# A hybrid HGRN2 and gMLP block on 8 cores: gates taken a turn ahead, attention steps a group later, sums on GpSimd

## The chip, the cores and the metric

One Trainium2 chip, all 8 cores, one launch. Each core computes half a sequence (1024 of 2048 positions) of one of 4 batch rows. The time is the device time of the slowest core in microseconds.

## What is computed

```python
h = rmsnorm(x, norm_mix)
q, f_pre, inp, g, u, v, gate_a, gate_b = split(h @ w_in)      # 4 x 1024, 2 x 1024, 2 x 2048 columns
f = lb + (1 - lb) * sigmoid(f_pre)                            # HGRN2: 8 heads of 128, state 128 x 128
o = hgrn2_scan(silu(q), 1 - f, inp, log(f))                   # S_t = diag(f_t) S_{t-1} + k_t v_t^T, o_t = S_t^T q_t
y_a = (rmsnorm(o) * silu(g)) @ w_a_out
y_b = (gelu(u) * gmlp_spatial(layernorm(gelu(v)))) @ w_b_out  # W_s mixes 128 positions, 8 heads
x = x + (sigmoid(gate_a) * y_a + sigmoid(gate_b) * y_b) @ w_o
x = x + relu(rmsnorm(x) @ w_ff1) ** 2 @ w_ff2                 # 2048 -> 8192 -> 2048
x = x + sigmoid(rmsnorm(x) @ w_ple_gate) * (p @ w_ple_proj)
return rmsnorm(x)
```

A core with the second half of a sequence also needs the state at its start. It gets it from the first half's x (`xpT`, zeros on the other cores), whose forget gates and values it computes too.

## The kernel before

The program is written out by hand, engine by engine, with one semaphore per engine: `X.after(event)` is a wait until that event of engine X, and each engine carries out its own list strictly in order. Activations lie transposed, 16 chunks of 128 features by 1024 positions; a half `hf` is 512 positions. A matrix product is cut into groups of 16 matmuls (one per chunk `c`) that fill one of 8 PSUM banks of 128x512. Weights are stored as float32 and arrive as bfloat16 through GpSimd's DMA queue (`load`, L1135) in four slots of 4096 columns; a slot's next load waits until TensorE (PE) has used it (`frees`). The loads of x go through SyncE's queue.

The stages, in order:

- **Start.** x comes in 9 pieces (L1188). For each chunk VectorE (DVE) makes the bfloat16 product with the gain (`raw`, L852), ScalarE (ACT) squares each half into `SQ[hf]` (L626, one buffer per half), and DVE adds the square to `ACC` (`accumulate`, L843). PE runs the first 8 `u` groups chunk by chunk (L353) as x arrives, then the other 8 group by group; after the first of these come the two matmuls that sum the squares over partitions (`total("x", 4)`, L341). `rstd` (L635, L638) turns this into the norm factor. Then DVE writes the normalised x (`normalise`, L861, 32 pieces) and after every second piece scales one `u` group (`u_scale`, L871), in the order of `UG`, that is groups 0 to 7 first; ACT takes the gelu (L650). The `u` groups of n = 6, 7 reuse banks of n = 4, 5.
- **V.** 8 value groups `V(1, i)` and 8 `V(0, i)` from the normalised x (L409). During `V(1, i)` the first half's x lands, piece by piece after the normalised pieces 2i+1 of half 1, and is squared and summed as before. Then `total("xp")`, and `V(2, i)`.
- **Heads.** `mixer_order` writes a list that all engines walk through. Step X has 8 groups k (two each of fp, f, q, g for head X). Between them stand the small steps of the heads a = X-2 and b = X-1. At k = 4: `on` (sum of squares of the head's output, PE L491, in banks 4 and 5), `decay` (4 exponentials on ACT, 3 products on DVE), `onorm` (ln, exp, products; L719 to L723 on ACT), `logf` (2 logarithms, 2 scans of 2.3 us, L964 and L969). Then the transposes `tk`, `tkp` (L442), the masked products `attn` (masks on DVE, L992 and L994), `kv` (a chain of 7 small DVE products and 8 small GpSimd products, L1007 and L1157). The small steps take turns between banks 4 and 5, and each waits until the engine that reads the step two before it has freed the bank (`take`). In the list of ACT a step's copy stands where the step stands.
- **v groups.** Steps X = 8 and 9 have no head groups; their 16 places hold the v groups (i, a) of the gMLP, with `vn` (layer norm on DVE with a short hop to GpSimd: L1018, L1020, L1162, L1164, L1022) once both halves a of a position block i are there, `bt` (bias terms, PE L496, DVE L1033), and `sp` (spatial products, PE L380; DVE L917 and L923). Behind them follow `gate(0, 0, 0)`, `gate(0, 0, 1)`, 4 spatial steps of the second half, `gate(0, 1, 0)`, 4 more, `gate(0, 1, 1)`. The first of these spatial steps waits for `vn` of i = 7.
- **Merge, w_o, the MLP** (L442 to L572): not touched.
- **Last stage.** 32 turns t (half by half): PE does the 16 matmuls of `pg` (L597) and 2 of `pp`; DVE scales the gate (L1111), ACT takes the sigmoid (L814), DVE multiplies (L1114) and adds (L1117), ACT squares (L626), DVE sums (L843). DVE waits for the sigmoid in each turn. `finish` (L1098) scales the output, half 0 beside the turns of half 1, half 1 at the end, and SyncE stores it (L1203).

## Time and profile before

| | us |
|---|---|
| runs: median (lowest to highest) | 2046.86 (2044.54 to 2274.42), 3 runs |
| the profiled execution, its own time | 2047.13 |
| its span on the slowest core (5) | 2045.8 |
| spans of the 8 cores | 2033.6 to 2045.8 |
| busy in it: PE, DVE, ACT, GpSimd | 1947.7, 688.8, 573.1, 111.6 |

The span is the time from the first to the last instruction of a core; outside it lie 1.3 us of the execution's own time. The granted clock is the share of TensorE's full speed (2.4 GHz) that the chip allowed; 0.5 is its lower level (1.2 GHz). In the windows, a stretch whose PE is busy for less than its length has waits of PE in it.

### The profile page before, as it was taken

Reading aid. Unit: us, or ns where it says so; the run is one execution under the profiler, and the core shown is the slowest. Engines: PE = TensorE matmul, PEld = TensorE weight load, DVE = VectorE, ACT = ScalarE, POOL = GpSimd, SP = SyncE. Lnnn points to the kernel's source line nnn. Section 1 sums busy time; section 2 is a strip of 40 time slices with the busy share of each in tenths; the row PEclk is TensorE's granted clock in tenths of the full one; section 3 lists DMA queues with packets and bytes.
Section 4 is the critical chain, followed back from the end, with each engine's and each line's share of the span. In section 5 each row is a group of like instructions: output and inputs, shape, how many; then the busy total and the mean of one; then the engine's idle time right before and its main releaser. Section 6 shows DMA issues by size and latency. Waiting matters only on the chain.

```text
span 2045.8 us, 25263 instructions; the slowest of 8 cores (2033.6 to 2045.8 us)
## 1 busy us (share of the span) xinstructions
PE 1947.7 (95%) x9300; PEld 891.6 (44%) x9300; DVE 688.8 (34%) x1042; ACT 573.1 (28%) x886; POOL 111.6 (5%) x235
## 2 busy tenths in 40 slices
PE   5799989998899999999999999999999999999993
PEld 2344444444444444444444444444444444444441
DVE  4760455246531222223312122121222112233667
ACT  3453465445211111123432003300231013333332
POOL 1000001011100000000000000000000000000000
PEclk9899999999899999999999999999999999999997
DMA  9851314142374434354434434434443444563304
GB/s 223 180 126 31 62 32 73 27 83 52 52 177 102 91 64 85 70 124 83 73 72 83 79 68 81 83 68 77 83 74 71 82 81 76 101 124 67 58 21 144
DMA packets 33127, 174.04 MB, mean 85 GB/s; under 512 B 3056, under 2 KB 3184, under 8 KB 18032
## 3 DMA queue, kind: packets, MB, share of 16 engines
q0 software_dynamic: 21872, 138.16, 37.3%
q1 hardware_dynamic: 11136, 34.26, 5.2%
q8 instruction: 78, 1.28, 0.3%
q14 instruction: 41, 0.34, 0.1%
HBM read 302.17 MB, written 8.39 MB: 152 GB/s over the span
## 4 chain that ended last, share of the span: by engine, by line
PE 87%; DVE 4%; DMA 3%; ACT 3%; issue 2%; SPq 0%; DVEq 0%; ACTq 0%; POOL 0%; POOLq 0%
PE ps L572 49%; PE ps L333 27%; PE ps L409 5%; DMA RX<-xT 2%; PE ps L597 2%; PE ps L432 2%; DMA RW<-wb 1%; DVE RX L1098 1%; DVE RP L1114 1%; ACT RP L814 1%; DVE RC L843 1%; DVE RH L861 1%; DVE RP L1111 0%; PE ps L442 0%; ACT L708 0%
## 5 line engine op out<-in xcount | busy, mean ns | idle before, releaser
L572 PE MATMUL ps<-RH,RW 128*128 128x512 bf16 x2048 | 442.8, 379 | 0.0
L333 PE MATMUL ps<-RH,RW 128*128 128x512 bf16 x1792 | 409.9, 383 | 5.7 <-DMA RW<-wb 5.7
L572 PE MATMUL ps<-RP,RW 128*128 128x512 bf16 x1536 | 332.0, 379 | 0.0
L572 PEld LDWEIGHTS ps<-RH,RW 128*128 128x128 bf16 x2048 | 200.4, 98 | 241.6
L333 PEld LDWEIGHTS ps<-RH,RW 128*128 128x128 bf16 x1792 | 175.4, 99 | 213.5 <-issue 14.1
L1071 DVE TENSOR_TENSOR RX<-RX,ps 128x512 f32<-128x512 f32 x160 | 110.1, 688 | 406.5 <-PE ps L572 406.5
L572 PEld LDWEIGHTS ps<-RP,RW 128*128 128x128 bf16 x1536 | 150.3, 98 | 181.2
L572 PE MATMUL ps<-RQ,RW 128*128 128x512 bf16 x1024 | 221.3, 379 | 0.0
L800 ACT ACTIVATE ps<-ps 128x512 f32<-128x512 f32 x128 | 74.5, 582 | 502.8 <-PE ps L572 502.8
L1089 DVE TENSOR_TENSOR ps<-ps,RC 128x512 f32<-128x512 f32 x128 | 89.6, 700 | 353.2 <-ACT ps L800 353.2
L626 ACT ACTIVATE RC<-RX 128x512 bf16<-128x512 f32 (+1 forms) x160 | 99.3, 629 | 259.4 <-DVE RC L843 226.4
L1135 POOL DMA_DIRECT2D RW<-wb x136 | 73.3, 540 | 1698.5 <-PE ps L572 924.5
L572 PEld LDWEIGHTS ps<-RQ,RW 128*128 128x128 bf16 x1024 | 100.2, 98 | 120.8
L333 PE MATMUL ps<-RQ,RW 128*128 128x512 bf16 x512 | 120.5, 379 | 0.0
L774 ACT ACTIVATE RX<-ps 128x512 f32<-128x512 f32 x64 | 38.2, 597 | 290.2 <-PE ps L333 290.2
L843 DVE TENSOR_TENSOR RC<-RC 128x512 f32<-128x512 f32 x150 | 100.1, 685 | 6.2 <-ACT RC L626 6.2
L333 PE MATMUL ps<-RP,RW 128*128 128x512 bf16 x384 | 87.8, 386 | 13.0 <-ACT RQ L650 11.5
L333 PEld LDWEIGHTS ps<-RQ,RW 128*128 128x128 bf16 x512 | 50.1, 98 | 60.4
L1051 DVE TENSOR_TENSOR RX<-RX,ps 128x512 f32<-128x512 f32 x32 | 22.0, 688 | 136.5 <-PE ps L333 136.1
L333 PEld LDWEIGHTS ps<-RP,RW 128*128 128x128 bf16 x384 | 37.4, 99 | 57.5 <-issue 16.7
L432 PE MATMUL ps<-RW,RH 128*128 128x512 bf16 x256 | 59.5, 387 | 1.3 <-DMA RW<-wb 1.3
L1048 DVE TENSOR_TENSOR RX<-RX,ps 128x512 f32<-128x512 f32 x32 | 22.0, 688 | 110.5 <-PE ps L333 110.5
(135 smaller groups left out, 1301.0 us busy)
## 6 DMA issues: line engine op xcount, KB each, us to landing
RW<-wb POOLq DMA_DIRECT2D x112, 1024.0 KB, 8.0
RW<-wb POOLq DMA_DIRECT2D x24, 512.0 KB, 10.1
RX<-xT SPq DMA_DIRECT2D x8, 1024.0 KB, 33.2
RX<-xpT SPq DMA_DIRECT2D x8, 1024.0 KB, 13.1
outT<-RX SPq DMA_DIRECT2D x16, 512.0 KB, 4.0
RX<-xT SPq DMA_DIRECT2D x2, 2048.0 KB, 18.4
RX<-xT SPq DMA_DIRECT2D x2, 1536.0 KB, 39.4
RP<-wb POOLq DMA_DIRECT2D x3, 1024.0 KB, 13.5
```

What stands on the lines that cost most here:

```text
L333: ins = e.matmul(out, w3[:, c, cs], src[:, c, ts], start=c == 0, stop=c == kc - 1)
L409: ins = e.matmul(PS[bank][:, :], src[:, c, i * 128:(i + 1) * 128], wide[c // 8][:, c % 8, :], start=c == 0, stop=c == 15)
L432: ins = e.matmul(PS[bank][:, :], HT[:, c, i * 128:(i + 1) * 128], wide[c // 8][:, c % 8, :], start=c == 0, stop=c == 15)
L572: ins = e.matmul(PS[b + hf][:, :], w3[:, c, (n % 2) * 128:(n % 2 + 1) * 128], src[:, c, half(hf)], start=c == 0, stop=c == 15)
L597: ins = e.matmul(PS[b][:, :], w3[:, c, (n % 2) * 128:(n % 2 + 1) * 128], HT[:, c, half(hf)], start=c == 0, stop=c == 15)
L626: e.activation(out=SQ[hf] if n else ACC[:, half(hf)], in_=XT[:, n, half(hf)], func=AF.Square, scale=D ** -0.5).then_inc(*ACT.on("sq", tag, ...
L774: e.activation(out=TMPA[2 * g + k], in_=PS[b0 + 2 * k][:, :], func=AF.Sigmoid).then_inc(*ACT.on("sg" + name, n, hf))
L800: e.activation(out=pb, in_=pb, func=AF.Relu).then_inc(*ACT.on("relu", q, n, hf))
L843: e.tensor_tensor(out=SQ[hf] if n == 15 else acc, in0=acc, in1=SQ[hf], op=ALU.add).then_inc(*DVE.on("acc", tag, n, hf))
L1071: e.tensor_tensor(out=XT[:, n, half(hf)], in0=XT[:, n, half(hf)], in1=PS[b_of(n) + hf][:, :], op=ALU.add).then_inc(*DVE.on("xadd", tag, n, ...
L1089: e.tensor_tensor(out=pb, in0=pb, in1=RSTD[:, half(hf)], op=ALU.mult).then_inc(*DVE.on("hr", q, n, hf))
L1135: e.dma_start(out=c3(WS[j % NSLOT][:, 0:n], 2048), in_=c3(wb_d[blk][:, 0:n], 2048)).then_inc(*WL[j % NSLOT].on("w", j))
```

## The change

- **Last stage:** the gate's scaling and its sigmoid are issued one turn ahead, on DVE and on ACT. Three `finish` that stood behind the turns go into turns 28 to 31, the sum of half 0 is totalled a turn later, and ACT calls a logarithm before its last wait.
- **Start:** the first two weight blocks are cut by rows (1024 rows by 512 columns), so that they are loaded in 4 transfers instead of 8. The sums of half 1 of x run on GpSimd. Blocks 2 and 3 are issued after GpSimd's tenth sum instead of upon x's chunks 10 and 11, block 2 in two halves. `total("x")` stands before the second 8 `u` groups and waits for GpSimd. The `u` groups are scaled in a new order (`U_TURN`: the first is group (4, 0)), one after each of the first 16 normalised pieces.
- **V:** the first half's x is squared beside `V(0, i)` instead of `V(1, i)`, and its total stands after `V(2, 0)`.
- **Heads:** `tk`, `tkp`, `spre` stand one group later, `attn(b, 0)` directly behind `tkp`; `kv`, `intra` and `inter` go in pairs; at k = 4 the order is `ek` (the first exponential), `oln` (the logarithms of `onorm`), the rest of `decay`, the rest of `onorm`, `logf`.
- **v groups:** the values go four by four (i = 0 to 3 with a = 0, then a = 1, then i = 4 to 7), with four buffers instead of two; `bt` stands at places 6 and 7 instead of 2 and 3, and `sp` at 9, 10 and 12 to 15.

```diff
@@ weight_blocks, mixer_order @@
-    for j in range(4):
+    for k in range(2):
+        blks.append(("w_in", k * 1024, 1024, [(4096, 512)]))
+    for j in range(2, 4):
         blks.append(("w_in", 0, D, [(4096 + j * 256, 256)]))
...
-    values = [(0, 0), (1, 0), (0, 1), (1, 1)] + [(i, a) for i in range(2, 8) for a in range(2)]
+    values = [(i + j, a) for i in (0, 4) for a in range(2) for j in range(4)]
...
-                out += [[("attn", a, 1), ("kv", a, 0)], [("kv", a, 1), ("intra", a, 0)], [("intra", a, 1), ("inter", a, 0)],
-                        [("inter", a, 1), ("sqo", a)], [("on", a)], [], [], []][k]
+                out += [[("spre", a), ("attn", a, 1)], [("kv", a, 0), ("kv", a, 1)], [("intra", a, 0), ("intra", a, 1)],
+                        [("inter", a, 0), ("inter", a, 1), ("sqo", a)], [("on", a)], [], [], []][k]
             if k == 4:
+                if 0 <= b < NH:
+                    out.append(("ek", b))
+                if 0 <= a < NH:
+                    out.append(("oln", a))
...
-                out += [[], [], [], [], [], [("tk", b)], [("tkp", b)], [("spre", b), ("attn", b, 0)]][k]
+                out += [[], [], [], [], [], [], [("tk", b)], [("tkp", b), ("attn", b, 0)]][k]
...
-                if g in (2, 3):
-                    out.append(("bt", g - 2))
-                if g >= 9:
-                    out += [("sp", g - 9, 0)] + [("sp", 7, 0)] * (g == 15)
+                if g in (6, 7):
+                    out.append(("bt", g - 6))
+                out += [("sp", h, 0) for h in {9: (0,), 10: (1,), 12: (2,), 13: (3, 4), 14: (5, 6), 15: (7,)}.get(g, ())]
@@ emit @@
-    BT = rxf(2048)
+    BT = rxf(6144)
-    GVT = [RP[:, 4096 + i * 2048:4096 + (i + 1) * 2048].bitcast(F32) for i in range(2)]
+    GVT = [RP[:, 4096 + i * 2048:4096 + (i + 1) * 2048].bitcast(F32) for i in range(2)] + [rxf(5120), rxf(2048)]
+    U_TURN = [g for pair in zip(UG[8:], UG[4:8] + UG[:4]) for g in pair]
@@ pe_program @@
-                e.wait_ge(*DVE.after("acc", tag, 15, hf))
+                e.wait_ge(*(POOL if tag == "x" and hf else DVE).after("acc", tag, 15, hf))
...
             for n, hf in UG[:8]:
-                w3 = c3(slot("u", n // 2), 256)
-                ins = e.matmul(PS[BANK["u", n, hf]][:, :], w3[:, c, (n % 2) * 128:(n % 2 + 1) * 128], RPv[:, c, half(hf)],
+                ins = e.matmul(PS[BANK["u", n, hf]][:, :], w3[:, c % 8, n * 128:(n + 1) * 128], RPv[:, c, half(hf)],
...
+        total("x", 0)
+        for n, hf in UG[8:]:
...
+                if (n, hf) == (4, 0) and c % 8 == 0:
+                    e.wait_ge(*U2L[c // 8].after("w"))
...
-            if k == 0:
-                total("x", 4)
...
-                if grp == 2 and i == 0:
+                if grp == 2 and i == 1:
                     total("xp", 6)
...
-                if (n, hf) == (1, 1):
+                if (n, hf) == (2, 1):
                     total("pg", 6, (0,))
@@ act_program @@
+        for n, hf in UG[:4]:
+            raw_u(n, hf)
+        rstd("x", 0, RSTDH)
+        for n, hf in UG[4:8]:
+            raw_u(n, hf)
+        for n, hf in U_TURN:
...
-                if grp == 1:
+                if grp == 0:
                     e.wait_ge(*XPL[i].after("x"))
...
+            elif kind == "ek":
...
                 e.activation(out=EK, in_=BBM, func=AF.Exp, scale=-1.0).then_inc(*ACT.on("ek", h))
+            elif kind == "decay":
...
+            elif kind == "oln":
...
-                if i >= 2:
-                    e.wait_ge(*DVE.after("vn", i - 2))
+                if i >= 4:
+                    e.wait_ge(*DVE.after("vn", i - 4))
+                elif (i, a) == (2, 0):
+                    e.wait_ge(*DVE.after("khtp", 6))
...
+        def sigmoid(t):
+            e.wait_ge(*DVE.after("gt1", t % 16, t // 16))
+            e.activation(out=GT[t % 2], in_=GT[t % 2], func=AF.Sigmoid).then_inc(*ACT.on("gts", t % 16, t // 16))
+
+        sigmoid(0)
...
+                if t < 31:
+                    sigmoid(t + 1)
                 e.wait_ge(*DVE.after("xadd", "pg", n, hf))
                 square("pg", n, hf)
...
+        e.activation(out=MISC[:, 3:4], in_=EPSC, func=AF.Ln).then_inc(*ACT.on("ln_table"))
         rstd("pg", 6, RSTDH, ("gt1", 15), (1,))
@@ dve_program @@
-            for hf in range(2):
-                if c >= 2:
-                    accumulate("x", c - 1, hf)
-        for hf in range(2):
-            accumulate("x", 15, hf)
+            if c >= 2:
+                accumulate("x", c - 1, 0)
+        accumulate("x", 15, 0)
...
-                if c % 2:
-                    u_scale(*todo.pop(0))
+                if hf == 0:
+                    u_scale(*U_TURN[c])
...
-                if c:
-                    accumulate("xp", c, hf)
+                if c >= 3:
+                    accumulate("xp", c - 2, hf)
+        for c in (14, 15):
+            for hf in range(2):
+                accumulate("xp", c, hf)
...
+        def gate(t):
+            n, hf = t % 16, t // 16
+            gt = GT[t % 2]
+            e.wait_ge(*PE.after("pg", n, hf))
+            if t >= 2:
+                e.wait_ge(*DVE.after("xadd", "pg", (t - 2) % 16, (t - 2) // 16))
+            e.tensor_tensor(out=gt, in0=PS[((16 * 9 + t) % 3) * 2][:, :], in1=RSTD[:, half(hf)], op=ALU.mult).then_inc(
+                *DVE.on("gt1", n, hf))
...
+        gate(0)
+        for t in range(32):
...
+            if t < 31:
+                gate(t + 1)
+            e.wait_ge(*ACT.after("gts", n, hf))
+            e.wait_ge(*PE.after("pp", n, hf))
...
+            if t >= 20:
+                finish(t - 20, 0)
+            if t >= 28:
+                finish(t - 16, 0)
+        accumulate("pg", 15, 1)
         for c in range(16):
             finish(c, 1)
@@ pool_program, sp_program @@
+        def accumulate_x(n):
+
+            e.wait_ge(*ACT.after("sq", "x", n, 1))
+            if n >= 2:
+                e.wait_ge(*POOL.after("acc", "x", n - 1, 1))
+            e.tensor_tensor(out=SQ[1] if n == 15 else ACC[:, 512:1024], in0=ACC[:, 512:1024], in1=SQ[1], op=ALU.add).then_inc(
+                *POOL.on("acc", "x", n, 1))
...
-            for j in range(2):
-                e.dma_start(out=WS[j][:, cols], in_=wb_d[j][:, cols]).then_inc(*UL[j][p].on("w"))
-        e.wait_ge(*XL[piece_of(11)].after("x"))
-        for j in range(2, 8):
+            cols = slice((p % 2) * 2048, (p % 2 + 1) * 2048)
+            e.dma_start(out=WS[p // 2][:, cols], in_=wb_d[p // 2][:, cols]).then_inc(*UL[p].on("w"))
+        for n in range(1, 11):
+            accumulate_x(n)
+        for p in range(2):
+            cols = slice(p * 2048, (p + 1) * 2048)
+            e.dma_start(out=WS[2][:, cols], in_=wb_d[2][:, cols]).then_inc(*U2L[p].on("w"))
+        load(3)
+        for n in range(11, 16):
+            accumulate_x(n)
+        for j in range(4, 8):
             load(j)
...
-        e.wait_ge(*DVE.after("khtp", 6))
+        e.wait_ge(*DVE.after("kt", 7))
         e.dma_start(out=BT, in_=bass.AP(bsp_d.tensor, 0, [[0, 128], [1, 1024]])).then_inc(*BSPL.on("bsp"))
```

## Rows read from the trace of the kernel before

**Rows 1.** The profile's page: busy time, share of the span and instructions of each engine
```profile
PE 1947.7 (95%) x9300; PEld 891.6 (44%) x9300; DVE 688.8 (34%) x1042; ACT 573.1 (28%) x886; POOL 111.6 (5%) x235
```
**Rows 2.** Windows: stretch, length, then busy time of each engine, clock, DMA
```profile
54.50:101.80 47.30, 34.24 (x147) 14.69 (x148) 34.78 (x54) 20.45 (x33) 1.59 (x3) 0.86 0.83 180
...
516.00:572.00 56.00, 46.62 (x272) 23.11 (x269) 33.32 (x57) 14.29 (x21) 8.66 (x21) 0.91 0.33 57
...
2013.00:2045.80 32.80, 0.80 (x2) 0.10 (x1) 22.84 (x35) 6.38 (x9) 0.00 (x0) 0.58 0.54 192
```
**Rows 3.** Waits of PE, whole span: us in total, times, longest
```profile
PE ps L442 <- ACT RC L719: 13.2, 5, 2.9
PE ps L333 <- ACT RQ L650: 11.5, 1, 11.5
...
PE ps L333 <- DMA RW<-wb: 5.7, 1, 5.7
```
**Rows 4.** Timeline of the start: start, us, engine, line [idle before <- releaser]
```profile
41.22 0.75 DVE L852 TENSOR_SCALAR RP<-RX,RC 128x1024 bf16<-128x1024 f32 x1 [2.30 <-DMA RX<-xT]
...
44.22 1.07 POOL L1135 DMA_DIRECT2D RW<-wb  x2 [38.26 <-DMA RX<-xT]
...
57.00 1.23 ACT L626 ACTIVATE RC<-RX 128x512 bf16<-128x512 f32 x2 [0.63 <-DVE RC L843]
...
59.84 3.61 PE L333 MATMUL ps<-RP,RW 128*128 128x512 bf16 x16 [1.50 <-ACT RQ L646]
```
**Rows 5.** Timeline, normalised pieces and the wait in the u groups
```profile
67.45 1.42 DVE L861 SCALAR_TENSOR_TENSOR RH<-RX,RC 128x512 bf16<-128x512 f32 x2 [8.35 <-ACT RC L638]
...
85.72 6.58 PE L333 MATMUL ps<-RP,RW 128*128 128x512 bf16 x20 [11.48 <-ACT RQ L650]
```
**Rows 6.** GpSimd's own operations by source line: ns min/median/max
```profile
L1157 POOL TENSOR_SCALAR RX<-RX x64: 371/372/380, 245.9 to 524.5; 128x128 bf16<-128x128 f32 x64
...
L1162 POOL TENSOR_TENSOR RC<-RC x8: 184/189/192, 495.3 to 555.7; 128x1 f32<-128x1 f32 x8
```
**Rows 7.** Timeline of a head step, from its group k = 4
```profile
259.96 0.59 PE L491 MATMUL ps<-RC 128*128 128x512 bf16 x2
...
260.83 1.28 ACT L708 ACT_TABLE_LOAD   x1
...
266.87 0.55 PE L442 MATMUL ps<-RC,RX 128*128 128x128 bf16 x7 [2.87 <-ACT RC L719]
...
267.26 5.30 PE L333 MATMUL ps<-RH,RW 128*128 128x512 bf16 x16
...
271.73 0.91 ACT L747 ACTIVATE RX<-ps 128x896 bf16<-128x896 bf16 x1
```
**Rows 8.** Timeline of the v groups: the on step, a vn on DVE, the last gate
```profile
498.39 0.61 PE L491 MATMUL ps<-RC 128*128 128x512 bf16 x2 [2.17 <-DVE RX L1033]
...
505.65 1.28 DVE L1018 BATCH_NORM_STATS2 RC<-RP 128x6 f32<-128x512 f32 x2
...
508.37 0.81 DVE L1022 TENSOR_SCALAR RP<-RP,RC 128x1024 bf16<-128x1024 f32 x1 [1.13 <-POOL RC L1164]
...
571.76 3.40 PE L333 MATMUL ps<-RH,RW 128*128 128x512 bf16 x15
```
**Rows 9.** Timeline of the last turns and the end
```profile
2012.65 0.68 DVE L1111 TENSOR_TENSOR RP<-ps,RC 128x512 f32<-128x512 f32 x1
...
2014.23 0.69 DVE L1114 TENSOR_TENSOR RP<-RP,ps 128x512 f32<-128x512 f32 x1 [0.90 <-ACT RP L814]
...
2016.96 0.68 DVE L1111 TENSOR_TENSOR RP<-ps,RC 128x512 f32<-128x512 f32 x1
...
2025.90 0.69 DVE L843 TENSOR_TENSOR RC<-RC 128x512 bf16<-128x512 f32 x1 [0.23 <-ACT RC L626]
...
2030.55 10.69 DVE L1098 SCALAR_TENSOR_TENSOR RX<-RX,RC 128x512 f32<-128x512 f32 x16 [1.97 <-ACT RC L638]
```

76 lines of the change are left out of this document (32 added, 44 removed).

## The prediction

> **What bounds the kernel now.** The page first: PE is busy for 1947.7 of 2045.8 us [rows 1], so about 98 us can be had at most, and the matmuls themselves are untouched. Then the windows, to see where PE waits: 13.1 us of 47.3 between 54.5 and 101.8, 9.4 between 516 and 572, and 32.0 behind the last turn [rows 2]. The waits of PE give the causes: a bank that a gelu has not freed (11.5), the attention transposes that wait for the logarithms of `onorm` (5 times, 13.2 in all), one late weight block (5.7) [rows 3]; the timeline adds 2.17 for `bt` ahead of `on` at X = 8 [rows 8]. Half as dear again is the clock: after a wait of 2.87 us a group took 5.30 instead of 3.61 [rows 7], after the one of 11.48 us 20 matmuls took 6.58 [rows 5] where 16 take 3.61 and 15 take 3.40 [rows 4, 8], which makes 0.215 a matmul and 3.45 from one group's start to the next; that wait cost 6.58 - 20 x 0.215 = 2.3 us more. All sums below are made on the profiled execution (2047.1, 1.3 of it outside the span), which lies 0.3 above the median of the runs.
>
> **Last stage.** A turn takes DVE 2016.96 - 2012.65 = 4.31 us; in it the second product starts 1.58 us after the first because the sigmoid lies between [rows 9]. PE needs 18 matmuls, 3.88, so DVE falls behind through half 1. With the sigmoid a turn ahead the product follows after about 0.64 (two instructions of 512 columns that wait for nothing take 1.28, [rows 8]) and the turn takes 4.31 - 1.58 + 0.64 = 3.37: DVE keeps up, and turns 28 to 31, which take a `finish` (0.67, 16 in 10.69) more, are 0.15 over PE, 0.4 us in all. PE's last gate ends at about 2012.6, as DVE had been waiting for no one. From there stand before the last sum: scaling 0.64, product 0.86, add 0.64, sum 0.64, two `finish` 1.34, then product 0.86, add 0.64, sum 0.64, two `finish` 1.34, together 7.6, so it starts at 2020.2 + 0.4 instead of 2025.90 [rows 9]. The early logarithm takes a table load of 1.28 [rows 7] off what follows. The 16 `finish` and the last store stay. **Gain 6.6**; the ends are 0 (the new order makes the product of turn t wait for the matmuls of t + 1, and ACT could trail) and 8.
>
> **Start.** The wait of 11.48 [rows 5] goes: group (4, 0) is now scaled first, straight after the first normalised piece, and its bank is asked for only 4 groups (13.8 us) after the total, while the path from total to normalise takes about 4 and scaling and gelu with table 0.7 + 1.3 + 0.6 more. DVE has the same 48 instructions, in another order; V's first group needs the 16th piece 31 us after the total, and DVE, which now waits for PE's u groups in between, has it at 30. So nothing is late there. The wait and its slow clock are worth 11.5 + 2.3 = 13.8.
>
> New is GpSimd's chain. ACT may not square the next chunk's half 1 before GpSimd has added the last one (one buffer). A square takes 0.6 (two in 1.23, [rows 4]). GpSimd's addition of two 512 inputs is not in the trace. Its own operations take 189 ns for one element and 372 for 128 [rows 6], so one input of 512 would take 0.93, two read in turn 1.66: I take 1.3, the middle. With two hand-overs a chunk costs 2.15. From chunk 8, whose x is there at 41.2 [rows 4], 8 chunks take 17.2, and three DMA issues between additions 10 and 11 take 3 x 0.53 (two take 1.07, [rows 4]): the total can start at 60.0, after 0.5 of hand-over and matmul at 60.5, where PE before began group (4, 0) at 59.84 [rows 4]. DVE, freed of half the sums, lets PE finish the first 8 groups some 2 us earlier, but PE then only waits longer, about 4 us, and is slow afterwards (2). Net of the start: 13.8 - 0.7 - 2 = 11.1. Ends: with 0.93 an addition, 3 more; with 1.66, 3 less. The weights' first transfers carry the same bytes before the same chunk, and blocks 2 and 3 no longer press on the last x; the issue of block 2 moves from 44.2 to about 48, and it is needed at 60.5, hidden if it lands in 12 us: taken at 0, from -2 to +1.
>
> The Trainium skill (GPSIMD Engine Reference, section 3.1) puts an fp32 addition of two tensors at 1.96 times DVE's; with this trace's 0.69 that would be 1.35, and the sum would stay where it is. The same skill (SBUF — State Buffer, section Who interferes with whom) says that GpSimd shares a pair of ports with DVE and is shut out by some DVE instructions altogether; that speaks against this edit, and is the first rival.
>
> **V.** The squares of the first half's x now start with `V(0, 0)` and must be through by the end of `V(2, 0)`. A chunk costs DVE one product of 0.75 [rows 4] and two sums, 0.64 each, near 1.9 us, so 14 chunks take 26 to 27 from the first; 8 V groups take 27.6. The last two cannot start before ACT's copy of `V(0, 7)`. I get the total 1.5 us late: **-1.5**. The loads of that x start later but end at the same time, and are needed 20 us later.
>
> **Heads.** The transpose's wait goes: `oln` stands before three exponentials and the transpose a group later. But ACT's burst behind k = 4 is what it was: from the group's start at 259.96 to the copy of `tk` 11.8 us [rows 7]. Now also the copy of q's second half stands before `tk`'s (0.5 more, with 0.4 for `khtp`, which is late by the moved logarithms): it ends at 259.96 + 12.6 + 0.91 = 13.6 after the start. And `attn(b, 0)` takes the same bank as `tk`: the steps alternate between two banks and it is the second after. PE is there after 0.43 + 3 x 3.45 + 0.84 = 11.6. So PE waits 2.0 us, and once more 0.65 for `attn(b, 1)`, whose bank DVE frees behind its two scans. Old waits at five steps: 13.2 with 4.5 of slow clock (5.30 - 3.61 = 1.7 in [rows 7], some 1.4 each behind the two others of that length); new: 5 x 2.65 = 13.3 with little slow clock. Gain 4.4, ends 0 (slow clock again) and 17.7 (no new wait). The smaller old waits of the first head and of V(3) (3.3 together) give 1.1 more after a new one of 1.5. **Gain 5.5**.
>
> **v groups.** The late block goes (it is now asked for 4 groups earlier), as do the waits for `bt` and one for v's weights. But DVE has a queue: at X = 8, from k = 4, three products end at 7.9, `onorm` and its product at 10.5, then `vn(0)` and `vn(1)`. One `vn` takes 508.37 + 0.81 - 505.65 = 3.5, since DVE waits in it for GpSimd [rows 8]. `bt(0)` (four small products, some 1.1) stands behind them and is done at 10.4 + 2 x 3.45 + 1.1 = 18.4. `attn(7, 0)` takes `bt(0)`'s bank, and PE is there at 11.8: a new wait of 6.6 us. Later, groups 12 to 15 take PE 15 us but give DVE four `vn`, six `sp` (a product and one that depends on it, 0.64 + 0.86 = 1.5 each) and an `onorm`, 25 us; so PE waits about 1 us at three `sp` steps and 3.5 for `vn(7)` before the second half's spatial steps. Before, gate(0, 1, 1) began at 571.76 [rows 8], 75.5 after the point where PE first stood at `on` (498.39 - 2.17 = 496.2); by this chain it begins 76 to 77 after it, and before that point a short wait for weights (1.3) is gone. **Gain 0**, ends -5 and +15.
>
> **Sum.** 6.6 + 11.1 - 1.5 + 5.5 + 0 = 21.7; 2047.1 - 21.7 = 2025. Its own range, from the ends that are not rivals: 2017 to 2032.
>
> **Rivals.**
> 1. DVE blocks GpSimd's additions. For it: both run at once in just this stretch, DVE 0.75 + 0.69 a chunk. Against: the trace has them together only on small tiles. An addition then waits up to 1.44, a chunk costs 3.6, and from chunk 8 the total comes at 41.2 + 8 x 3.6 + 1.6 = 71.6: 11.6 us later, **2037**. That is what the page's rule on the shared ports would do.
> 2. No new waits: I have the banks' turns or the queues wrong, and the heads give 17.7 + 3.3 and the v groups 15. For it: it is what the order looks made for; against: the sums of rows 7 and 8. Gain 11 + 7 - 1.5 + 21 + 15: **1995**.
> 3. The last stage gives nothing, since DVE is held by PE's next group each turn and ends as late: the change doesn't do there what it says. **2032**.
> 4. Slower: GpSimd's chain, long enough to eat all. Everything else gains 22; the chain must then end 22 us later, at 82, which takes (82 - 42.8) / 8 = 4.9 a chunk from chunk 8 on, an addition of 4.0 us. From there on the kernel is slower; at 5 us it is **2055**. Nothing in the rows is near that.
>
> **How the numbers follow.** Forecast 0.50, rival 1 0.22, rival 2 0.14, rival 3 0.10, rival 4 0.04. The range 2005 to 2037 leaves out most of rivals 2 and 4. About 2% is what a measurement of this kernel can tell from no change; faster by that means under 2006, which only rival 2 gives: 0.13. Slower by over 2% is over 2088: 0.01. Within: 0.86.
>
> **What would show it.** Right: no PE wait for a gelu near 75; a wait of PE for GpSimd's or ACT's sum before the total, at 56 to 60; PE waits at `attn` for ACT's `tk` copy, about 2 us in five steps; one of 6 to 7 us at `attn(7, 0)` for `bt`; the end 26 us after PE's last gate instead of 33. Wrong: an addition on GpSimd over 1.7 us (rival 1), PE without waits between 230 and 560 (rival 2), turns on DVE still 4.3 us apart (rival 3).

## The result, and the profile after

| | us |
|---|---|
| runs after: median (lowest to highest) | 2026.90 (2026.47 to 2027.48), 4 runs |
| ratio to the kernel before, 95% interval | 0.9908 [0.9884, 0.9932] |
| the profiled execution, its own time; span (core 3) | 2026.71; 2025.1 |
| spans of the 8 cores | 2021.2 to 2025.1 |

The kernel became 0.9% faster, 19 to 20 us, which is less than the 2% that count as a difference here. The forecast was 2025.0. Some runs of these kernels are disturbed, with the cores of one die or both at a lower clock, and take 2% or more longer; all times and ratios of this part leave them out.

The page's busy times after the change. The work is that of [rows 1], but 15 additions went from DVE to GpSimd and ACT has one logarithm more:

```profile
PE 1942.8 (96%) x9300; PEld 890.7 (44%) x9300; DVE 690.7 (34%) x1027; ACT 573.1 (28%) x887; POOL 127.4 (6%) x247
```

The gain is too small to be read from that. The waits of PE show where it went (us in total, times, longest); they answer to [rows 3]:

```profile
PE ps L471 <- ACT RX L766: 13.2, 6, 2.5
PE ps L361 <- DMA RW<-wb: 11.4, 1, 11.4
PE ps L361 <- DVE RP L880: 11.3, 12, 7.4
PE ps L350 <- DVE RC L871: 10.1, 3, 8.2
PE ps L471 <- DVE RX L1062: 6.7, 1, 6.7
PE ps L392 <- DVE RP L1051: 3.9, 1, 3.9
...
PE ps L471 <- DVE RX L1023: 1.2, 5, 0.2
```

The gelu wait (11.5), the late weight block (5.7) and the transposes' wait for `onorm` are gone. New are `attn` for the copy of `tk` (L766, 13.2), `attn` for `bt` (L1062, 6.7) and the spatial step for `vn(7)` (L1051, 3.9).

Five points that PE passes in both traces cut the two spans into six stretches. The first columns compare the slowest core before (5) with the slowest after (3), the last one the averages over all eight cores of the same two executions:

| stretch, by PE's position | before | after | gain | forecast | gain, average of 8 cores |
|---|---|---|---|---|---|
| start, to the first group of `V(1, 0)` | 101.6 | 85.6 | 16.0 | 11.1 | 13.7 |
| V, to `fp(0, 0)` | 83.5 | 87.5 | -4.0 | -1.5 | -2.9 |
| heads, to `v(0, 0)` | 294.1 | 287.7 | 6.4 | 5.5 | 5.5 |
| v groups, to `gate(0, 1, 1)` | 92.5 | 95.6 | -3.1 | 0 | -3.3 |
| from there to PE's last gate | 1441.4 | 1441.3 | 0.2 | 0 | 5.0 with the next |
| from that to the end | 32.6 | 27.5 | 5.1 | 6.6 | |
| sum (of unrounded values) | 2045.8 | 2025.1 | 20.7 | 21.7 | 17.9 |

The slowest core is not a typical one. Before, `V(1, 0)` starts at 96.4 to 103.2 on the eight cores (101.6 on core 5, since its x came late), afterwards at 84.8 to 85.6; the average core gained 17.9 us, the slowest 20.7.

The windows of three of these stretches answer to [rows 2] (columns as there). From 54 to 85.6 PE is busy for 30.17 of 31.60 us at full clock, where it had lost 13 us of 47; the stretch around `attn(7, 0)` is no better than before (47.87 of 56); the last one is shorter, and its DMA share is higher (0.74 over 27.5 us, 0.54 over 32.8 before):

```profile
54.00:85.60 31.60, 30.17 (x139) 13.40 (x140) 20.06 (x31) 18.40 (x30) 3.98 (x5) 1.00 0.90 142
...
500.00:556.00 56.00, 47.87 (x276) 23.92 (x275) 35.15 (x63) 14.00 (x21) 8.93 (x22) 0.94 0.35 57
1997.60:2025.10 27.50, 0.61 (x2) 0.10 (x1) 18.39 (x29) 4.69 (x7) 0.00 (x0) 0.57 0.74 229
```

**The start.** The timeline of the last input sums and of the two matmuls of the total. The last addition starts at 56.35 and is followed by the matmul for half 1 at 57.65; PE waited 1.04 and 0.39 us for the two matmuls. Group (4, 0) begins at 57.97, where the forecast had 60.5 and a wait of 4:

```profile
54.18 1.24 POOL L1174 TENSOR_TENSOR RC<-RC 128x512 f32<-128x512 f32 x1 [0.93 <-ACT RC L638]
...
56.35 1.15 POOL L1174 TENSOR_TENSOR RC<-RC 128x512 bf16<-128x512 f32 x1 [0.93 <-ACT RC L638]
...
57.65 0.38 PE L350 MATMUL ps<-RC 128*128 128x512 bf16 x1 [0.39 <-ACT RQ L658]
...
85.60 4.70 PE L421 MATMUL ps<-RW,RH 128*128 128x512 bf16 x21
```

**V, heads and v groups.** PE's timeline again. At 146.22 the total of the first half's x waits for its last sum, and the 15 matmuls behind it take 5.08 us (granted clock 0.67 from 147.2 to 152.3). At 261.16 `attn` waits 2.16 for the copy of `tk`, and the group behind it runs at full speed (3.62 for 16). At 494.59 `attn(7, 0)` waits 6.71 for `bt(0)` and at 548.45 the spatial step waits for `vn(7)`; the groups behind these take 5.77 and 5.51 (granted clock 0.62 and 0.65):

```profile
146.22 0.38 PE L350 MATMUL ps<-RC 128*128 128x512 bf16 x1 [1.75 <-DVE RC L871]
...
147.24 5.08 PE L421 MATMUL ps<-RW,RP 128*128 128x512 bf16 x15
...
261.16 0.38 PE L471 MATMUL ps<-RX 128*128 128x128 bf16 x4 [2.16 <-ACT RX L766]
261.38 3.62 PE L342 MATMUL ps<-RH,RW 128*128 128x512 bf16 x16
...
494.59 0.58 PE L471 MATMUL ps<-RX 128*128 128x128 bf16 x4 [6.71 <-DVE RX L1062]
494.97 5.77 PE L444 MATMUL ps<-RW,RH 128*128 128x512 bf16 x16
...
548.45 1.86 PE L392 MATMUL ps<-RP 128*128 128x128 bf16 x16 [3.89 <-DVE RP L1051]
550.11 5.51 PE L342 MATMUL ps<-RH,RW 128*128 128x512 bf16 x16
```

Two of these slow stretches are not to be found on every core. Core 0 has the same waits in the same execution (1.75 and 0.23; 3.51 for `vn(7)`), but its clock stays at 1.00 behind both: 27 matmuls take 5.99 from 147.21, and the group behind `vn(7)` takes 3.62:

```profile
547.21 3.62 PE L342 MATMUL ps<-RH,RW 128*128 128x512 bf16 x16
```

Behind the total of the first half's x the clock falls on cores 3, 5 and 7 (V takes 87.4 to 87.5 us there, 85.8 on the other five), behind `vn(7)` on cores 3 and 7 alone (v groups 95.6 and 95.7, 93.3 to 93.6 on the other six). These two cores end last, at 2025.1 and 2024.8. Behind the 6.7 us for `bt` it falls on all eight.

**The end.** DVE's last sum starts at 2004.96 and the 16 last `finish` start at 2008.32. PE's last gate ended at 1997.62, so they start 10.7 us behind it, where [rows 9] had 2030.55 - 2013.2 = 17.3. The span ends 6.1 us after the last of them (2008.32 + 10.69), before 4.6:

```profile
2004.96 0.68 DVE L871 TENSOR_TENSOR RC<-RC 128x512 bf16<-128x512 f32 x1
2008.32 10.69 DVE L1127 SCALAR_TENSOR_TENSOR RX<-RX,RC 128x512 f32<-128x512 f32 x16 [2.67 <-ACT RC L650]
```

### The profile page after: what moved, and what is told of

Read it like the earlier page. It is cut to its first block, busy times and chain, and to the rows that moved or that the text cites. A ratio compares the mean times of both kernels' runs of the same rounds, so it can differ in the third digit from the quotient of the medians.

```text
span 2025.1 us, 25256 instructions; the slowest of 8 cores (2021.2 to 2025.1 us)
## 1 busy us (share of the span) xinstructions
PE 1942.8 (96%) x9300; PEld 890.7 (44%) x9300; DVE 690.7 (34%) x1027; ACT 573.1 (28%) x887; POOL 127.4 (6%) x247
## 3 DMA queue, kind: packets, MB, share of 16 engines
q0 software_dynamic: 21440, 138.16, 38.5%
## 4 chain that ended last, share of the span: by engine, by line
PE 87%; DVE 6%; issue 3%; ACT 2%; DMA 1%; POOL 0%; DVEq 0%; SPq 0%; ACTq 0%; POOLq 0%
PE ps L584 49%; PE ps L342 24%; PE ps L609 5%; PE ps L421 4%; PE ps L444 2%; PE ps L378 1%; DMA RX<-xT 1%; DVE RC L871 1%; DVE RX L1127 1%; DVE RX L998 0%; DVE RX L993 0%; DVE RP L880 0%; ACT L725 0%; DVE RC L1047 0%; DVE RX L978 0%
## 5 line engine op out<-in xcount | busy, mean ns | idle before, releaser
L584 PE MATMUL ps<-RH,RW 128*128 128x512 bf16 x2048 | 442.8, 379 | 0.0
L342 PE MATMUL ps<-RH,RW 128*128 128x512 bf16 x1792 | 404.7, 380 | 0.0
L584 PE MATMUL ps<-RP,RW 128*128 128x512 bf16 x1536 | 332.0, 379 | 0.0
L584 PEld LDWEIGHTS ps<-RP,RW 128*128 128x128 bf16 x1536 | 150.3, 98 | 181.2
L871 DVE TENSOR_TENSOR RC<-RC 128x512 f32<-128x512 f32 x135 | 92.0, 692 | 16.9 <-ACT RC L638 16.9
L421 PE MATMUL ps<-RW,RP 128*128 128x512 bf16 x256 | 58.4, 387 | 0.0
L609 PE MATMUL ps<-RH,RW 128*128 128x512 bf16 x256 | 57.9, 379 | 0.0
```

Source lines behind the costliest of these rows:

```text
L342: ins = e.matmul(out, w3[:, c, cs], src[:, c, ts], start=c == 0, stop=c == kc - 1)
L421: ins = e.matmul(PS[bank][:, :], src[:, c, i * 128:(i + 1) * 128], wide[c // 8][:, c % 8, :], start=c == 0, stop=c == 15)
L584: ins = e.matmul(PS[b + hf][:, :], w3[:, c, (n % 2) * 128:(n % 2 + 1) * 128], src[:, c, half(hf)], start=c == 0, stop=c == 15)
L609: ins = e.matmul(PS[b][:, :], w3[:, c, (n % 2) * 128:(n % 2 + 1) * 128], HT[:, c, half(hf)], start=c == 0, stop=c == 15)
L871: e.tensor_tensor(out=SQ[hf] if n == 15 else acc, in0=acc, in1=SQ[hf], op=ALU.add).then_inc(*DVE.on("acc", tag, n, hf))
```

## The experiments

All start from the changed kernel (2026.9) and compute the whole of the reference. They were measured on three occasions, each with its own runs of the kernel before: the sums back on DVE, the early logarithms, `vn` in two parts and the old order of the scalings beside a median of 2048.6, the two with the earlier half 0 beside 2045.9, the others beside 2047.2. The ratios refer to these runs; for the changed kernel's own the median is 2045.7. So times of different occasions can be compared to some 3 us only. The averages over the eight cores of each profiled execution, stretch by stretch, are steadier: where an edit leaves a stretch alone, it agrees with the changed kernel's to 0.6 us, in the v groups to 1.0 (2.0 with the early logarithms). In us, with the two last stretches of the table above as one:

| | start | V | heads | v groups | rest |
|---|---|---|---|---|---|
| before | 98.9 | 83.5 | 293.6 | 90.7 | 1474.3 |
| the changed kernel | 85.2 | 86.4 | 288.1 | 94.0 | 1469.3 |
| input sums back on DVE | 81.7 | 87.0 | 288.3 | 93.7 | 1469.2 |
| logarithms early | 85.5 | 86.6 | 283.7 | 96.0 | 1468.7 |
| the same, minus part first | 85.8 | 86.8 | 274.4 | 94.2 | 1468.9 |
| `vn` in two parts | 85.7 | 86.4 | 288.4 | 84.8 | 1468.7 |
| the old last stage | 85.7 | 86.4 | 288.7 | 94.0 | 1475.2 |
| half 0 scaled earlier | 85.5 | 86.9 | 288.2 | 95.0 | 1466.3 |
| four edits together | 81.3 | 83.5 | 275.0 | 82.5 | 1469.2 |
| the same, half 0 earlier | 81.3 | 83.5 | 274.9 | 83.1 | 1466.2 |

### Input sums back on DVE

```diff
-            if c >= 2:
-                accumulate("x", c - 1, 0)
+            for hf in range(2):
+                if c >= 2:
+                    accumulate("x", c - 1, hf)
...
-        for n in range(1, 11):
-            accumulate_x(n)
+        e.wait_ge(*DVE.after("acc", "x", 10, 1))
```

> The changed kernel with the sums of half 1 of x back on DVE (block 2 is issued after DVE's tenth sum). Changed kernel: 2026.9. Theory (GpSimd shuts DVE out: the gain product takes 1.64 us instead of 0.75 while an addition of GpSimd's runs, so a chunk costs 2.16 us and TensorE is fed at that pace): a chunk costs 1.87 again, over some 11 chunks 3.2 us, the total comes at about 54 instead of 56.9, time 2024. Rival, as the prediction had it (GpSimd's sums let TensorE finish the first groups about 2 us earlier, at a price only for the total): no gain or a loss, 2027 to 2029.

Measured: **2023.96** (2022.77 to 2025.20), ratio to before 0.9882 [0.9863, 0.9901]. So moving half of the sums to GpSimd cost 2.9 us by the medians. That is near the spread, but the start is not: `V(1, 0)` begins at 80.6 to 82.9 us on the eight cores, with the sums on GpSimd at 84.8 to 85.6, 3.5 us later on average. The rows say why. First the gain product of the changed kernel by its source line (ns min/median/max, then the first and the last start):

```profile
L880 DVE TENSOR_SCALAR RP<-RX,RC x16: 740/1641/2411, 6.3 to 52.2; 128x1024 bf16<-128x1024 f32 x16
```

Its group in the table by lines, from 25 to 57 us (busy us, mean ns), 13 of the 16:

```profile
L880 DVE TENSOR_SCALAR RP<-RX,RC 128x1024 bf16<-128x1024 f32 x13 | 19.4, 1495 | 1.5 <-DMA RX<-xT 1.5
```

And one meeting of the two engines in the timeline:

```profile
49.84 1.25 POOL L1174 TENSOR_TENSOR RC<-RC 128x512 f32<-128x512 f32 x1 [0.93 <-ACT RC L638]
50.01 1.64 DVE L880 TENSOR_SCALAR RP<-RX,RC 128x1024 bf16<-128x1024 f32 x1
```

The same product by its source line, and then the timeline, of the kernel with the sums on DVE:

```profile
L880 DVE TENSOR_SCALAR RP<-RX,RC x16: 748/751/754, 7.8 to 50.2; 128x1024 bf16<-128x1024 f32 x16
```

```profile
48.35 0.75 DVE L880 TENSOR_SCALAR RP<-RX,RC 128x1024 bf16<-128x1024 f32 x1
...
50.22 0.75 DVE L880 TENSOR_SCALAR RP<-RX,RC 128x1024 bf16<-128x1024 f32 x1
```

The product takes 0.75 us each time when GpSimd adds nothing, and 1.64 when it starts 0.17 after an addition. The 13 products lose 19.4 - 13 x 0.75 = 9.7 us, about what DVE was spared by 14 sums of 0.69. In the steady chunks the balance is against GpSimd: a product lasts 0.89 us longer, and a sum less brings 0.60 from start to start. A chunk costs 2.17 with GpSimd (54.18 to 56.35) and 1.87 without (48.35 to 50.22).

### The logarithms of a head before the attention groups

```diff
-                if X < NH:
-                    out.append(("logf", X))
+            if k == 2 and 0 <= b < NH:
+                out.append(("logf", b))
```

> The changed kernel with the two logarithms and scans of a head (logf) moved from group 4 of its own step to group 2 of the next step, so that they no longer stand between onorm and the copy of tk on ACT, nor in front of the masks on DVE. Changed kernel: 2026.9. Theory (attn(b, 0) waits for ACT's copy of tk because ACT's burst is too long, and attn(b, 1) for masks behind the scans): the six waits for L766 (13.2 us) and the five for the masks (1.2) go, some slow clock with them, time 2012 to 2014. Rival (the burst only moves: two more table loads a head and the scans then hold up ek, inter or the forget gates): waits of the same size elsewhere, time 2024 to 2028.

Measured: **2023.6** (2023.14 to 2024.61), ratio 0.9879 [0.9850, 0.9908]. The theory missed by 10 us; the time is that of the rival. The waits of PE first, then a row of ACT's timeline:

```profile
PE ps L471 <- ACT RX L766: 6.0, 5, 1.6
...
PE ps L471 <- DVE RQ L989: 1.4, 1, 1.4
```

```profile
249.38 1.28 ACT L725 ACT_TABLE_LOAD   x1 [2.52 <-DVE RX L1007]
```

The wait for `tk`'s copy fell from 13.2 to 6.0 and small waits took its place; on the average of the cores the heads gain 4.4 us and the v groups lose 2.0. The burst on ACT now starts 2.52 us late: `ek` needs `wl` (L1007), which stands on DVE behind both scans. ACT waits for it in seven of the eight heads, 17.9 us in all (the expectation of the next experiment says 1.3 for one).

### The same, with the minus part first

On top of the last edit `logf` takes the two logarithms in the other order on ACT, and on DVE the scan of BBM and `wl` come before the scan of BBP (each with its own waits):

```diff
-                e.activation(out=BBP, in_=SGP[h % 2], func=AF.Ln, scale=OML[:, h:h + 1], bias=LB[:, h:h + 1]).then_inc(
-                    *ACT.on("lnp", h))
                 e.activation(out=BBM, in_=SGM[h % 2], func=AF.Ln, scale=OML[:, h:h + 1], bias=LB[:, h:h + 1]).then_inc(
                     *ACT.on("lnm", h))
+                e.activation(out=BBP, in_=SGP[h % 2], func=AF.Ln, scale=OML[:, h:h + 1], bias=LB[:, h:h + 1]).then_inc(
+                    *ACT.on("lnp", h))
```

> The head's logarithm is moved ahead of the two attention groups as in the run that moved it, and in addition ScalarE and VectorE take lnm, the scan and wl before lnp and its scan, so that wl is ready one scan (about 2.4 us) sooner and ek does not wait for it. My theory: the 13.2 us of TensorE waiting for the copy of tk at attn(b,0) are a matter of order on ScalarE and VectorE. In the earlier run ek waited 1.3 us for wl, so the copy was still late. With wl sooner the waits for the copy come to 2 us or less in all, and the time is 2013 to 2015. Rival: the head's work on the two engines is simply too much for the stretch, and the waits move to another place as they did in the earlier run: 2024, with a sum of the new waits in the heads of 10 us or more.

Measured: **2013.5** (2011.47 to 2014.43), ratio 0.9836 [0.9820, 0.9851]. ACT's timeline of the same step, then PE's: `ek` starts without a wait (its table load at 245.35), the copy of `tk` (L766) ends at 255.2, and `attn` (L471) follows at 256.39 without one. Among the waits of PE L766 is gone, and `on` waits four times for its square, 0.9 us together:

```profile
254.25 0.92 ACT L766 ACTIVATE RX<-ps 128x896 bf16<-128x896 bf16 x1
```

```profile
256.39 0.39 PE L471 MATMUL ps<-RX 128*128 128x128 bf16 x4
```

So the 13.2 us were a matter of order, not of load: 13.4 us came back (13.7 in the heads by the average of the cores), 10.1 of them through the order of the two logarithms and scans.

### `vn` in two parts

```diff
-                if g and values[g - 1][1]:
-                    out.append(("vn", values[g - 1][0]))
+                out += {6: [("bt", 0), ("vs", 0)], 7: [("vn", 0), ("bt", 1)], 8: [("vs", 1), ("vs", 2), ("vn", 1)],
+                        9: [("vs", 3), ("vn", 2)], 10: [("vn", 3), ("sp", 0, 0)], 11: [("sp", 1, 0)], 12: [("sp", 2, 0)],
+                        13: [("vs", 4), ("sp", 3, 0)], 14: [("vn", 4), ("vs", 5), ("sp", 4, 0), ("sp", 5, 0)],
+                        15: [("vn", 5), ("vs", 6)]}.get(g, [])
+    out += [("vs", 7), ("vn", 6), ("vn", 7), ("sp", 6, 0), ("sp", 7, 0)]
```

`vs` is the statistics on DVE and GpSimd's hop, `vn` the scaling alone. Whatever DVE does between the two hides the hop.

> The changed kernel with each vn split in two list entries (statistics; normalisation one entry or more later), so that DVE works on while GpSimd takes the root, with bt(0) ahead of all vn and vn(7) ahead of the last two sp. Changed kernel: 2026.9. Theory (DVE's queue is what TensorE waits for in the v groups: 6.7 at attn(7, 0), 1.1, three of 3.1 together, 3.9 before the second half's spatial steps, and about 4 us of slow clock behind the two long ones): waits of 2 to 3 us in all are left, time 2011 to 2014. Rival (only the bank of bt matters, the end of the stretch stays bound by DVE): 6.7 + 2 go, time 2018.

Measured: **2016.2 to 2017.4** (three runs), ratio 0.9848 [0.9826, 0.9870], median 2017.4: 9.5 us, 3 short of the theory and nearer to the rival's 2018. But the rival has the reason wrong: the end of the stretch is no longer bound by DVE as it was. The longest wait of PE that is left in the v groups is for a `vn` (L1053); `bt` (L1064) has 1.1 left of 6.7, and the 3.9 for `vn(7)` are gone:

```profile
PE ps L391 <- DVE RP L1053: 1.7, 1, 1.7
```

All waits of the stretch come to 6.7 us (14.8 before), where the theory had 2 to 3, and of the slow clock 1.6 us stay: behind that wait 15 matmuls take 4.96 us from 510.62, at a granted clock of 0.67. That is why the theory's time was not reached. What DVE was doing during the wait for `bt` stands in its timeline of the changed kernel: two `vn`, each with more than a microsecond in which it does nothing but wait for GpSimd, and then `bt` (L1062):

```profile
492.49 0.81 DVE L1051 TENSOR_SCALAR RP<-RP,RC 128x1024 bf16<-128x1024 f32 x1 [1.13 <-POOL RC L1216]
493.21 1.12 DVE L1062 SCALAR_TENSOR_TENSOR RX<-ps,RC,RX 128x128 f32<-128x128 f32 x4
```

### The old order of the `u` scalings

```diff
-    U_TURN = [g for pair in zip(UG[8:], UG[4:8] + UG[:4]) for g in pair]
+    U_TURN = UG
...
-                if hf == 0:
-                    u_scale(*U_TURN[c])
+                if c % 2:
+                    u_scale(*U_TURN[8 * hf + c // 2])
```

> The changed kernel with the u groups scaled in the old order (groups 0 to 15, one after every second normalised piece), the total still ahead of the second eight groups. Changed kernel: 2026.9. Theory (the order of scaling is what removed TensorE's wait for the gelu): the bank wait is back, but 3.8 us shorter than before because the total now comes one group earlier, 7.7 us, with 2 us of slow clock: 2036 to 2037. Rival (the earlier total alone did it): 2027.

Measured: 2036.1, in a single run, as expected. PE's timeline has the wait back, with slow matmuls behind it. The two cost 8.15 + 10.33 - 35 x 0.215 = 11.0; PE's waits for the gain product are 2.0 less in this run (9.3 instead of 11.3), which leaves 9.0 of the 9.2 us:

```profile
79.91 10.33 PE L378 MATMUL ps<-RP,RW 128*128 128x512 bf16 x35 [8.15 <-ACT RQ L667]
```

### The old last stage

The core of the edit, of ACT's list and DVE's:

```diff
-                if t < 31:
-                    sigmoid(t + 1)
+                e.wait_ge(*DVE.after("gt1", n, hf))
+                e.activation(out=GT[t % 2], in_=GT[t % 2], func=AF.Sigmoid).then_inc(*ACT.on("gts", n, hf))
...
-            if t < 31:
-                gate(t + 1)
...
-            if t >= 28:
-                finish(t - 16, 0)
```

> Only the last stage is as before: gate and sigmoid of a turn within the turn, no early loading of the Ln table, finishes one turn later. Read from the two profiles, the stretch after TensorE's end went from 32.6 to 27.6 us, so my theory says 2026.9 + 5.1 = 2032.0 (the last finish starts 17.9 us after TensorE's end, and the last store lands 4.6 us after the last finish, not 6.1). Rival: what the last stage gained is lost again in the stores, which are bunched at the end either way, so that the old order costs nothing: 2027.

Measured: **2034.65** (2032.49 to 2035.84), ratio 0.9943 [0.9925, 0.9960]. DVE's timeline has the old gap of 0.90 in a turn again, and the last `finish` start 2015.51 - 1998.44 = 17.1 us after PE's last gate; the span ends 4.7 us after them:

```profile
1999.47 0.69 DVE L1135 TENSOR_TENSOR RP<-RP,ps 128x512 f32<-128x512 f32 x1 [0.90 <-ACT RP L835]
...
2015.51 10.69 DVE L1120 SCALAR_TENSOR_TENSOR RX<-RX,RC 128x512 f32<-128x512 f32 x16 [1.69 <-ACT RC L650]
```

By the profiled executions (2032.49 against 2026.71) the new last stage is worth 5.8 us, by the medians 7.8. The trace accounts for 5.8: 5.0 behind PE's last gate and 0.8 by which that gate ends later, 0.3 of it a wait of PE for a gate's bank (L1132). The remaining 2 lie within the spread of the runs: from `gate(0, 1, 1)` on, the average over the eight cores is 5.9 us longer (1475.2 against 1469.3), and no core of one kernel reaches into the range of the other.

### The first weights by columns

```diff
-            cols = slice((p % 2) * 2048, (p % 2 + 1) * 2048)
-            e.dma_start(out=WS[p // 2][:, cols], ...)
+            for j in range(2):
+                e.dma_start(out=WS[j][:, cols], ...)
```

> Only the first weights are loaded by columns again, eight transfers, and the products wait for both blocks of a row group. In the profile after the change the first product starts 4.8 us sooner, at 11.4 and not at 16.2, but from the ninth chunk TensorE is fed by the scaling and GpSimd's sums at 2.16 us a chunk, which would hide a late start. My theory: the row cut is worth nothing by itself, 2027 (2026 to 2028). Rival: the earlier start moves VectorE's chain with it, and the row cut brought some 3 us: 2030.

Measured: **2026.9** (2026.44 to 2028.52), ratio 0.9905 [0.9887, 0.9922]. The row cut gains nothing that can be seen. `V(1, 0)` begins at 84.7 to 87.0 us on the eight cores, with the row cut at 84.8 to 85.6. PE's first wait is 13.9 us with it undone and 11.4 with the change, but kernels with the same cut and the same start have 11.8 to 14.1 there, so that difference isn't the cut's. PE is held afterwards by the scaled chunks: 10.6 us in 9 waits here, 11.3 in 12 there.

```profile
PE ps L360 <- DMA RW<-wb: 13.9, 1, 13.9
...
PE ps L360 <- DVE RP L879: 10.6, 9, 3.1
```

### Four edits together

The edits of the first, third and fourth experiment in one kernel, and with them

```diff
-                if grp == 2 and i == 1:
+                if grp == 2 and i == 2:
                     total("xp", 6)
```

> Four edits at once: input sums back on VectorE, minus part of the head's logarithm first and ahead of the two attention groups, normalisation of v split into statistics and scaling and spread over the steps, the input's total two products later. My theory: each of the waits that they remove is at its own place, and their gains add: 3 (sums) + 12 (copy of tk) + 11 (normalisation) + 2 (total) under 2026.9, so about 1999. Rival: the head part doesn't give its 12, since what remains of that wait is VectorE's load; then the sum is 3 + 3 + 11 + 2, so about 2008. Under 2002 speaks for the first, over 2006 for the second.

Measured: **1995.3** (1994.15 to 1995.94), ratio 0.9748 [0.9732, 0.9763]. The gains add. By the medians the four terms, with 2 estimated for the total, make 2.9 + 13.4 + 9.5 + 2 = 27.8, and 31.6 are measured. The averages over the cores tell where the rest comes from: against the changed kernel the start is 3.9 shorter (3.5 in its own experiment), V 2.9 (the total, estimated at 2; its slow clock went as well), the heads 13.1 (13.7) and the v groups 11.5 (9.2). Why the v groups give 2.3 more in this company is open. The largest waits of PE that are left:

```profile
PE ps L360 <- DMA RW<-wb: 12.7, 1, 12.7
PE ps L349 <- DVE RC L870: 8.2, 1, 8.2
PE ps L360 <- DVE RP L879: 6.0, 1, 6.0
```

They lie at the two ends of the kernel, where the input is awaited and the output is finished; the next one is 1.9 us.

### Half 0 scaled for the output earlier

```diff
-            if t >= 20:
-                finish(t - 20, 0)
-            if t >= 28:
-                finish(t - 16, 0)
+            if t in (20, 21, 22, 23):
+                finish(2 * (t - 20), 0)
+                finish(2 * (t - 20) + 1, 0)
+            elif t >= 24:
+                finish(t - 16, 0)
```

> Only the order in which the last stage scales its first half for the output changes: two chunks in each of the turns 20 to 23 and one in each from 24 to 31, where the change has one from 20 on and a second in the last four. In the profile after the change three of the first half's eight pairs are stored only after turn 31, so that the DMA engines are busy for 0.96 and 1.00 of the time from 2005 on, and the last store lands 6.1 us after the last scaling. My theory: with one pair left over there the last store lands 4.6 us after it, as before the change, and the time is 1.5 us less, 2025.4. Rival: the second half's own stores fill the DMA engines anyway, and the tail stays at 6.1 us: 2026.9. The stretch from the last scaling to the end of the span decides, 4.6 or 6.1 us, since the times lie closer than their spread.

Measured: **2024.78** (2024.54 to 2025.65), ratio 0.9898 [0.9883, 0.9913]. The same in the kernel with the four edits:

> The four edits together (input sums on VectorE, minus part first and early, statistics and scaling of v split, the input's total later), with the order of the last stage's scalings of the run above. My theory: 1995.3 less the 1.5 us of the stores, 1993.8, with 4.6 us from the last scaling to the end. Rival: the stores give nothing, 1995.3. Either way it is faster than the change as made by some 31 us, 1.5%.

Measured: **1992.1** (1990.11 to 1993.51), ratio 0.9737 [0.9722, 0.9751], the fastest version here, 1.7% below the change as made.

The time came as expected or a little better. The windows of the last 21.9 us, of the changed kernel and then of the one with the earlier half 0, show less to be moved at the end (264 and 216 GB/s):

```profile
2003.20:2025.10 21.90, 0.59 (x1) 0.10 (x1) 13.13 (x20) 3.43 (x5) 0.00 (x0) 0.50 0.87 264
```

```profile
2002.20:2024.10 21.90, 0.59 (x1) 0.10 (x1) 13.41 (x21) 3.44 (x5) 0.00 (x0) 0.50 0.65 216
```

DVE's last `finish` in the timeline of the latter:

```profile
2008.00 10.69 DVE L1127 SCALAR_TENSOR_TENSOR RX<-RX,RC 128x512 f32<-128x512 f32 x16 [2.68 <-ACT RC L650]
```

The stretch from the last scaling to the end, by which the expectation wanted to decide, can't be read from the slowest core alone: there it is 5.4 us, between the two values, and with the four edits 6.8 against 6.7 without the new order. Over the eight cores it reads clearly (us):

| last stage | from the last scaling to the end, average (lowest to highest) |
|---|---|
| before | 4.9 (3.7 to 6.8) |
| the changed kernel with the old last stage | 5.2 (4.2 to 7.2) |
| the changed kernel | 6.6 (6.0 to 7.3) |
| half 0 earlier | 4.8 (4.4 to 5.4) |
| four edits | 6.2 (5.3 to 7.4) |
| four edits, half 0 earlier | 5.0 (4.2 to 4.6 on six cores, 6.8 on two) |

So the theory holds: with less left to store at the end the last store lands 1.2 to 1.8 us sooner. To this comes 1.2 us on DVE, which the expectation did not have: PE's wait for the last sum falls from 8.16 to 6.96, since the last two turns, which end behind PE, have one `finish` each instead of two. Together it is 3.0 us from `gate(0, 1, 1)` on in both kernels (1469.3 to 1466.3 and 1469.2 to 1466.2). Without the four edits only 2.1 of them show in the medians; in that profiled execution the stretches V and v groups were slower by 0.5 and 1.0. Why single cores need up to 7.4 us is open.

## Why the prediction held, and where not

The total, 2025.0 against 2026.9, is close only because errors of both signs cancelled; that is luck. Three steps failed. First, the start: "the total can start at 60.0" took its anchor, x's chunk 8 at 41.2, from a core that was late, and "DVE, freed of half the sums, lets PE finish the first 8 groups some 2 us earlier" has the wrong sign; the total was there at 57.65, and with the sums back on DVE `V(1, 0)` begins 3.5 us sooner. Second, the new waits in V and in the v groups were priced without the slow clock behind them, which cost 5.9 us on the slowest core. Third, "the 16 `finish` and the last store stay": the last store lands 1.5 us later. By the stretches:

- **Last stage, 6.6; measured 5.1 from the last gate on, 5.8 by the profiled run with the old stage.** On the engines the step is exact: the last `finish` start 10.7 us behind PE's last gate instead of 17.3. The term "the 16 `finish` and the last store stay" failed: the last store lands 1.5 us later (1.7 on the average of the cores). The two versions with half 0 scaled earlier show the cause: three stores of half 0 are issued only at 2004.4 to 2006.3, with the earlier order one is, and there 1.8 and 1.2 us come back.
- **Start, 11.1; measured 16.0.** The wait for the gelu and its slow clock went as said (priced at 13.8 from the trace before; with the old scaling order in the changed kernel they came back at 11.0), and GpSimd's chain has the pace of the forecast (2.15 a chunk; 2.17 measured). The step that failed is the anchor: "the total can start at 60.0", counted from x's chunk 8 at 41.2. That time is core 5's, the slowest; on the other seven cores DVE took chunk 8 at 37.2 to 38.5. In the changed kernel it takes it at 35.5 to 36.3 and waits for x on no core, and GpSimd's eighth addition starts only at 40.43: from the fourth, at 31.85, the chain runs at its own pace and x no longer sets it. The three DMA issues cost it 0.8 us instead of 1.6. So the chain ended at 57.5, 2.5 us before the forecast, PE waited 1.4 us in all instead of 4, and no slow clock followed, which I had priced at 2; another 0.4 are the total's two matmuls, which had stood between group (4, 0) and the next.

```profile
36.25 1.64 DVE L880 TENSOR_SCALAR RP<-RX,RC 128x1024 bf16<-128x1024 f32 x1
```

Weight blocks 2 and 3 can't have delayed chunk 8 before the change: their loads were issued at 44.2, behind it. What they may have delayed is chunk 14, for which DVE waited on six of the eight cores before, and on none in the changed kernel, in the one with the sums on DVE or in the one with the weights by columns, which all ask for the two blocks later (no run moves these loads alone):

```profile
53.69 0.75 DVE L852 TENSOR_SCALAR RP<-RX,RC 128x1024 bf16<-128x1024 f32 x1 [1.10 <-DMA RX<-xT]
```

I had named this relief and taken it at 0. With the weights by columns DVE still waits for chunk 8, until 35.8 to 37.7; so the row cut brings the middle of x sooner, which the chain then hides.
- **Rival 1, DVE holding up GpSimd, was the right suspicion with the direction reversed.** GpSimd's addition takes 1.15 to 1.33 us in any company, and DVE's product pays (1.64 instead of 0.75). That also makes "DVE, freed of half the sums" wrong: it lost on the products more than it saved on the sums, and the edit costs 3.5 us at the start (2.9 in the time) instead of helping.
- **V, -1.5; measured -4.0.** The wait itself is right (1.75 and 0.23). Left out was the clock behind it: 15 matmuls in 5.08 us instead of 3.2, 1.9 more on core 3. On the five cores whose clock stayed up V takes 2.3 us more than before, 0.8 more than the forecast.
- **Heads, 5.5; measured 6.4.** The new waits are those of the forecast in place and cause, and near it in size: 13.2 us in six for ACT's copy of `tk` (forecast 2.0 in each of five), 1.2 in all for the masks (forecast 3.3), and groups at full clock behind them. The sum has a slip: the small waits give 3.3 - 1.5 = 1.8 and not 1.1, which makes 6.2 for the step. Rival 2, no new waits, fell; but the version with the minus part first shows that it describes what this order can give: without the new waits the kernel takes 2013.5.
- **v groups, 0; measured -3.1.** `bt`'s wait was forecast at 6.6 and is 6.71, `vn(7)`'s at 3.5 and is 3.89. Left out, again, was the clock behind the two: 5.77 - 3.62 and 5.51 - 3.62, 4.0 together on cores 3 and 7, and only the first of them on the other six. Core 5 before, to which the forecast compared, was slower here than the average as well (92.5 against 90.7).
- **Rivals 3 and 4** fell: a turn on DVE takes 3.9 to 4.0 us and not 4.3, and an addition 1.2 and not 4.

Two of the three terms that were too good have one fault: a new wait was priced by its length, though [rows 5] and [rows 7] had shown what the groups behind such a wait cost.

## What to carry to other kernels

Look up what stands before the wanted result in its engine's list, and move the result: the gain of 20 us became one of 55 by taking two scans in another order, by letting no engine stand in the list waiting for another's short hop, and by undoing one part that looked like pure relief. Work given to a second engine is no relief if it makes the first engine's other instructions longer; compare the duration of an untouched instruction before and after. A wait of PE is priced with the groups behind it, at the clock that the trace shows there, and that on all cores: the same wait was followed by full speed on some and by slow groups on others, and the slowest core is the one that had them. So is an anchor: a time taken from the slowest core alone can be that core's bad luck.
